# One decoder step on one core: the memory rows' squares added by VectorE in a tree, GpSimd's pooling sums behind the memory's 1/rms, seven stage slots

## What is computed

```python
h = rmsnorm(x, g_mix);  proj = h @ w_in            # columns: u (pool), q, k, v
u = proj[..., :512]
wsum[t] = sum(u[t-w+1 .. t])  for w in (2, 4, 8, 16)   # one window per 128 channels
d = wsum / count - u;  pool_out = (d @ w_pool) * s_pool
attn = softmax(q k^T) v                             # 8 heads of 64, rotary; paged cache for the 8 samples
x = x + concat(pool_out, attn) @ w_out
m = rmsnorm(memory, g_mem)                          # 256 memory rows: 1/rms = rsqrt(mean(memory^2) + eps)
mk = m @ w_ck;  mv = m @ w_cv
x = x + cross_attention(rmsnorm(x, g_cross) @ w_cq, mk, mv; cached mem_k, mem_v for the samples) @ w_co
x = x + relu(rmsnorm(x, g_mlp) @ w_up)^2 @ w_down
y = rmsnorm(x, g_final)
```

## Time and profile before

| | us |
|---|---|
| median of 3 runs | 417.19 (416.75 to 417.71) |
| the profiled execution, its own time | 417.26 |
| span of that execution in the trace | 415.2 |
| TensorE busy | 409.0 (99%) |
| VectorE busy | 253.1 (61%) |
| ScalarE busy | 226.7 (55%) |
| GpSimd busy | 31.9 (8%) |

### The profile page before, as it was taken

The page is one execution under the profiler, slowest core; times in us unless marked ns, Lnnn a source line. Parts: engine busy times, 40 slices in busy tenths (PEclk is TensorE's granted clock), DMA queues, the critical chain, the costliest instruction groups (busy, mean ns, idle before and its releaser), DMA issues.

```text
span 415.2 us, 8425 instructions
## 1 busy us (share of the span) xinstructions
PE 409.0 (99%) x3372; PEld 383.6 (92%) x3372; DVE 253.1 (61%) x400; ACT 226.7 (55%) x392; POOL 31.9 (8%) x41
## 2 busy tenths in 40 slices
PE   8999999999999999999999999999999999999995
PEld 8999979986879998957899999999999999999995
DVE  5899988576254796453259777766667534454302
ACT  5866957925364484424357666666565443453313
POOL 1004026000000120000022000000000000010010
PEclk9999999999999999999999999999999999999999
DMA  8999858974989968995537545655565555545002
GB/s 277 400 385 365 279 205 233 336 275 172 370 313 339 380 228 321 362 394 234 203 103 250 208 135 193 202 181 167 191 202 201 196 174 193 188 162 182 2 2 104
DMA packets 37257, 96.60 MB, mean 233 GB/s; under 512 B 4186, under 2 KB 13274, under 8 KB 37082
## 3 DMA queue, kind: packets, MB, share of 16 engines
q1 hardware_dynamic: 35106, 92.24, 63.5%
q10 hardware_dynamic: 2112, 3.82, 2.5%
HBM read 91.73 MB, written 4.54 MB: 232 GB/s over the span
## 4 chain that ended last, share of the span: by engine, by line
PE 85%; DVE 7%; DMA 4%; SPq 2%; issue 1%; ACT 1%; DVEq 0%
PE psum L1110 70%; PE psum L832 5%; DVE w_lo L1401 2%; PE psum L1052 2%; DMA raw<-in_w_in 2%; PE psum L960 2%; PE psum L947 2%; DMA pages<-in_page_table 1%; DMA raw<-in_w_ck 1%; SPq L778 1%; DVE mix_lo L1405 1%; PE psum L893 1%; PE psum L931 1%; ACT w_hi L1133 1%; PE psum L953 0%
## 5 line engine op out<-in xcount | busy, mean ns | idle before, releaser
L1401 DVE TENSOR_TENSOR w_lo<-raw,w_hi 128x1024 fp32r<-128x1024 f32 x67 | 82.6, 1243 | 61.0 <-ACT w_hi L1133 60.8
L1133 ACT ACTIVATE w_hi<-raw 128x1024 fp32r<-128x1024 f32 (+1 forms) x73 | 73.8, 1019 | 57.8 <-PE psum L1110 41.6
L1110 PE MATMUL psum<-mix_hi,w_hi 128*128 128x264 f32 (+1 forms) x288 | 82.4, 286 | 0.0
L1110 PE MATMUL psum<-mix_hi,w_lo 128*128 128x264 f32 (+1 forms) x288 | 81.1, 282 | 0.0
L1110 PE MATMUL psum<-mix_lo,w_hi 128*128 128x264 f32 (+1 forms) x288 | 81.1, 281 | 0.0
L1110 PE MATMUL psum<-act_hi,w_hi 128*128 128x264 f32 x232 | 66.5, 287 | 0.5 <-DVE w_lo L1401 0.5
L1110 PE MATMUL psum<-act_lo,w_hi 128*128 128x264 f32 x232 | 65.6, 283 | 0.0
L1110 PE MATMUL psum<-act_hi,w_lo 128*128 128x264 f32 x232 | 65.4, 282 | 0.0
L1110 PEld LDWEIGHTS psum<-mix_hi,w_hi 128*128 128x128 f32 x288 | 54.0, 188 | 1.0 <-issue 0.8
L1110 PEld LDWEIGHTS psum<-mix_lo,w_hi 128*128 128x128 f32 x288 | 54.0, 188 | 0.1
L1110 PEld LDWEIGHTS psum<-mix_hi,w_lo 128*128 128x128 f32 x288 | 54.0, 188 | 0.0
(11 more groups left out here) (208 smaller groups left out, 813.9 us busy)
## 6 DMA issues: line engine op xcount, KB each, us to landing
raw<-in_w_down SPq DMA_DIRECT2D x20, 512.0 KB, 3.3
raw<-in_w_up SPq DMA_DIRECT2D x18, 512.0 KB, 3.8
raw_more<-in_w_up SPq DMA_DIRECT2D x14, 512.0 KB, 3.7
stage<-in_mem_v SPq DMA_DIRECT2D x12, 512.0 KB, 6.6
raw_more<-in_w_down SPq DMA_DIRECT2D x12, 512.0 KB, 4.2
stage<-in_cache_v SPq DMA_DIRECT2D x16, 256.0 KB, 6.5
keysT<-in_cache_k SPq DMA_DIRECT2D x16, 256.0 KB, 5.4
keysT<-in_mem_k SPq DMA_DIRECT2D x8, 512.0 KB, 6.9
```

What stands on the lines that cost most here:

```text
L1110: mm = pe.matmul(out, a, b, start=first and m == 0, stop=end_ and m == 2)
L1133: return nc.scalar.activation(out, in_, ACT.Copy, scale=scale)
L1401: V.tensor_tensor(lo_of(c), raw_of(c), hi_of(c).bitcast(F32), ALU.subtract).then_inc(w_lo_ready, 1)
```

## The change

1. **Squares.** ScalarE writes the squares of the eight memory tiles into a new tile `m_squares` of eight places, with no wait for GpSimd. A new VectorE job `("sum_m",)` adds them in a tree of three instructions of 1024, 512 and 256 elements. It stands at chunk 16 behind the split. `("stat", "m")` moves from chunk 16 to chunk 17, and on ScalarE `("exp", 4)`, one head's exponentials, now comes ahead of it.
2. **GpSimd** no longer adds the memory's squares, and its four window sums wait for `rstd` of the memory (`rstd_ready` at 2) beside the take-out of the pooling columns.
3. **Seven stage slots.** All units from `V` 4 on move to another slot. The load `("mV", 1, 0, 3)` moves in SyncE's list from chunk 51 to the head of chunk 54's list, where it waits for `("xc_O", 0, 0)`, the first use of that half; `("mV", 0, 1, 3)` in the same list now waits for `("xc_O", 0, 1)`.
4. **`opart`** now lies over the constants `cos`, `sin`, `causal`, `head_q` and the pooling's counts, which have been used by then; the constants are stored in another order for this, and ScalarE's copy into it waits for the differences. With the freed slot this makes room for `m_squares`.

The core of the diff:

```diff
-STAGE = 8
+STAGE = 7
...
-    put(16, ("split",), ("stat", "m"), ("exp", 4))
-    put(17, ("m_lo", 7), ("split",))
+    put(16, ("split",), ("sum_m",), ("exp", 4))
+    put(17, ("stat", "m"), ("m_lo", 7), ("split",))
...
-    51: [("mV", 1, 0, 2), ("mV", 1, 0, 3), ("mK", 1, 2), ("mK", 1, 3)],
+    51: [("mV", 1, 0, 2), ("mK", 1, 2), ("mK", 1, 3)],
...
-    54: [("mV", 0, 1, 1), ("mV", 0, 1, 0), ("mV", 0, 1, 2), ("mV", 0, 1, 3), ("mV", 1, 1, 0), ("mV", 1, 1, 1), ("mV", 1, 1, 2), ("mV", 1, 1, 3)],
+    54: [("mV", 1, 0, 3), ("mV", 0, 1, 1), ("mV", 0, 1, 0), ("mV", 0, 1, 2), ("mV", 0, 1, 3), ("mV", 1, 1, 0), ("mV", 1, 1, 1), ("mV", 1, 1, 2), ("mV", 1, 1, 3)],
...
-        opart = sb("opart", [P, 2, CN], F32, early)
+        m_squares = sb("m_squares", [P, KT, MEM], F32, early)
+        opart = const[:, CONST_AT["cos"][0]:CONST_AT["cos"][0] + 2 * CN].rearrange("p (b n) -> p b n", b=2)
...
                     if i[0] == "x":
                         pe.wait_ge(x_summed, 1)
+                    elif i[0] == "m":
+                        pe.wait_ge(m_summed, 1)
                     else:
-                        pe.wait_ge(sq_added, (KT - 1) * m)
+                        pe.wait_ge(sq_added, (KT - 1) * (m - 1))
...
                     src = memory(k)
-                    square("m", k, src, MEM)
+                    nc.scalar.activation(m_squares[:, k, :], src, ACT.Square).then_inc(m_squared, 1)
...
+                    act.wait_ge(d_ready, len(WINDOWS))
                     copy(opart[:, OPART[job] % 2, :], B).then_inc(free, 1)
...
+                if what == "sum_m":
+                    dve.wait_ge(m_squared, KT)
+                    then(V.tensor_tensor(m_squares[:, 0:4, :], m_squares[:, 0:4, :], m_squares[:, 4:8, :], ALU.add))
+                    then(V.tensor_tensor(m_squares[:, 0:2, :], m_squares[:, 0:2, :], m_squares[:, 2:4, :], ALU.add))
+                    V.tensor_tensor(ssq[:, 1, 0:MEM], m_squares[:, 0, :], m_squares[:, 1, :], ALU.add).then_inc(m_summed, 1)
+                    return
...
-            add_squares("m")
-
             gp.wait_ge(pad_ready, 2)
             for f in range(AT):
                 wait_gemm_out(gp, group["in", 0], f)
             end_ = STATE + SEQ
+            gp.wait_ge(rstd_ready, 2)
```

More of the change, by code:

```diff
@@ L223 @@
 SCALED_BY_ACT = ()
-NO_PRODUCTS = ("m_tile", "m_lo", "differences", "square_x", "sum_x", "tables", "turn", "qblock", "k_out", "exp", "norm", "split")
+NO_PRODUCTS = ("m_tile", "m_lo", "differences", "square_x", "sum_x", "sum_m", "tables", "turn", "qblock", "k_out", "exp", "norm", "split")
 def plan_banks():
@@ L411, in host_constants @@
     parts = {
-        "cos": cos, "sin": sin, "ones": np.ones((P, P)), "eps": np.full((P, 1), EPS),
-        "causal": causal, "head_q": head_q, "head_x": head_x, "share": share,
-        "spread": spread, "inv_count": inv_count,
-        "inv_window": inv_window,
+        "ones": np.ones((P, P)), "eps": np.full((P, 1), EPS), "cos": cos, "sin": sin,
+        "causal": causal, "head_q": head_q, "inv_count": inv_count, "inv_window": inv_window,
+        "head_x": head_x, "share": share, "spread": spread,
         "ident": np.eye(P),
@@ L540, in build @@
         x_squared, x_summed = sem("x_squared"), sem("x_summed")
+        m_squared, m_summed = sem("m_squared"), sem("m_summed")
         rstd_ready, cols_ready = sem("rstd_ready"), sem("cols_ready")
@@ L1067, in sum_result @@
                 S, B = (psum[:, banks_of(len(GROUPS) - 1)[x], :] for x in (1, 2))
-                pe.wait_ge(sq_added, (KT - 1) * (m - 1) + KT - 2)
+                pe.wait_ge(sq_added, (KT - 1) * (m - 2) + KT - 2)
                 for t in range(2):
@@ L1072, in sum_result @@
                 turn_result(*Y_PARTS[0])
-                pe.wait_ge(sq_ready, KT * m)
+                pe.wait_ge(sq_ready, KT * (m - 1))
                 for t in range(2):
@@ L1147, in square @@
                 m = NORM[norm]
-                added = (KT - 1) * (m - 1) + max(k - SQ_SLOTS, 0)
+                added = (KT - 1) * (m - 2) + max(k - SQ_SLOTS, 0)
                 if added > 0:
                     act.wait_ge(sq_added, added)
-                if k == 0 and m >= 2:
+                if k == 0:
                     wait_full(act, ("stat", {2: "x", 3: "m", 4: "c"}[m]))
@@ L1690, in add_squares @@
                 m = NORM[norm]
-                n = MEM if norm == "m" else T
                 for k in range(1, KT - 1 if norm == "y" else KT):
-                    gp.wait_ge(sq_ready, KT * (m - 1) + k + 1)
+                    gp.wait_ge(sq_ready, KT * (m - 2) + k + 1)
                     if k > 1:
-                        gp.wait_ge(sq_added, (KT - 1) * (m - 1) + k - 1)
-                    nc.gpsimd.tensor_tensor(ssq[:, m % 2, 0:n], ssq[:, m % 2, 0:n], sq[:, k % SQ_SLOTS, 0:n], ALU.add).then_inc(sq_added, 1)
+                        gp.wait_ge(sq_added, (KT - 1) * (m - 2) + k - 1)
+                    nc.gpsimd.tensor_tensor(ssq[:, m % 2, :], ssq[:, m % 2, :], sq[:, k % SQ_SLOTS, :], ALU.add).then_inc(sq_added, 1)
             nc.gpsimd.memset(std[:, 0:P], 0.0).then_inc(warm_ready, 1)
```

## The result

The changed kernel takes 421.09 us, median of 4 runs (419.69, 421.04, 421.35 and 421.13 us), against 416.97 us for the kernel before in the same comparison: ratio 1.009, 95% interval 1.0073 to 1.0107. Slower, as forecast. But the median is 1.5 us above the 419.6 us predicted, and 0.1 us above the upper end of the range. (The kernel before was itself at 416.97 us here; the ratio of 1.009 on the forecast's 417.19 us would be 420.9 us.)

What follows compares the result with a forecast made beforehand. TensorE, busy for 99% of the span, was taken to bound the kernel. Terms of 0 - 0.3 + 2.1 + 0.6 = +2.4 us gave 419.6 us against the median of 417.19 us, range 418.4 to 421.0 us.

Steps and rivals of the forecast that it cites:

- What bounds the kernel: Whole kernel: TensorE, busy 99% of the span, bounds it; nothing after 57.65 us can absorb a delay of TensorE.
- GpSimd's adds go: TensorE's waits near 53 and 57.65 us: VectorE, no longer held up by GpSimd's adds, gains 0.3 us (0.2 to 0.4).
- The tree behind the split: Stat product behind chunk 17: TensorE waits for VectorE's tree behind chunk 20's split, a loss of 2.1 us (1.8 to 2.4).
- The rival without a wait: Stat product: tree done by 67.6 us, so TensorE does not wait and the kernel takes 416.9 us; chance 0.08.
- Behind the reciprocal: Chunk 20's second and third column blocks: splits alternating with window sums lose 0.15 and 0.45 us, together 0.6 (0 to 0.9).
- Seven slots and `opart`: Stage loads and ScalarE's copy into `opart`: the new waits cost 0 us, with an end at 1.0 us.
- The sum: Whole kernel: the terms add to +2.4 us, giving 419.6 us against the median of 417.19 us.
- my own sign: Behind the new wait: the forecast is wrong if TensorE's granted clock falls from 2.4 GHz; no price given.
- GpSimd first at the port: Behind the reciprocal: a window sum goes before `mix_lo` of tile 7, chunk 19 waits 1.8 us, 420.8 us; chance 0.13.
- the late load: At `xc_O(0,1)`: the moved load takes 6.0 us, not 4.7, a wait of 0.7 us, 420.3 us; chance 0.09.

Runs made afterwards that it cites:

- the first profile: Profile of the changed kernel's first of four runs against the kernel before: 419.69 us, span 417.2 us, TensorE at full clock throughout.
- the second set of runs: The changed kernel as it is, measured once more in more rounds against the kernel before: 421.75 us, ratio 1.0102.
- the long wait: The changed kernel with the memory's stat product back behind chunk 16, tree still behind the split of chunk 20: 424.43 us, ratio 1.0175.

## Why the prediction was right, and where it was not

**What bounds the kernel: right.** In the first profile TensorE's shift at 78 us is its shift at 409 us, and nothing behind absorbed or added anything. In two of the later profiles the next norm added 0.4 and 0.8 us.

**GpSimd's adds go: right, mis-sized.** 0.3 us were taken, 0.53 measured, which is also above the upper end of 0.4 us: 0.22 by the heads' transposes and the rest by O(0). That end counted the two waits that rows show. Two `w_lo` at 33 us take 2.36 us where they took 3.32, as worked out. The `uext` wait is gone, as said.

**The tree behind the split: right, and the one term that counts.** 2.1 us predicted at ends of 1.8 and 2.4, 2.05 us named by the trace, 2.30 us by the shift, so inside the ends by either. The working holds point by point: split 1.23 us, tree 2.41 us behind it, in the place that the sum gave it less the shift of 0.53 us. The rival without a wait needed the tree done by 67.6 us, 2.1 us earlier; among the kernels whose window sums still wait only those with the tree ahead of the split get there (66.15 us in the first), and that one takes 417.38 us where the rival had 416.9.

**Behind the reciprocal: right in its order, mis-sized.** `mix_lo` was first at the port, the two splits alternated with the sums. The second block lost 0.25 us (0.15 predicted). The third lost nothing (0.45 predicted). I had let the splits end at 78.75 us, less the shift 78.2, and they ended at 78.0; and I had put the third block 0.7 us behind the second, where it is 0.81 us, and TensorE came to the second 0.2 us later than in the sum. So the first `mkT` was 0.2 us early for it rather than late. Net 0.20 us in place of 0.6, inside the ends of 0 and 0.9.

**Seven slots and `opart`: right.** 0, by the run that has only these.

**The sum.** -0.53 + 2.30 + 0.20 = +1.97 us, where I had +2.4 us; with a further 0.4 us outside the span, which I had taken as unchanged, the profiled run is at 419.69 us where I had 419.7 us. Two errors of 0.4 us cancelled there.

**What the sum left out is what its last sentence names.** I named the granted clock as what would make me wrong and gave it no price, since the trace had no row at the other level. It fell in 7 of 9 runs and costs 1.5 us: by my own sign the forecast is wrong in these seven, and it is the fall that parts 419.6 us from 421.09 us (of the 2.15 us to 421.75 us it is the larger part). With a chance of its own for a fall, the range would have had to reach 422 us. As an estimate the figure could have been bounded from this case's rows: at half the clock the products of a stretch take as much again as the 0.12 us each that they took before (the profile of the second set of runs has 0.21 us), and only the length of the stretch was unknown. What I can't say even now is from the rows of before alone how likely a fall behind a wait of 2.1 us would be.

**The rivals.** GpSimd first at the port and the late load did not happen. The time that the former gave, 420.8 us, is near the measured one and for another reason.

## What to carry to other kernels

Place an addition in an in-order queue ahead of the instruction that still waits for a release: the same three instructions cost 2.3 us behind the split and nothing ahead of it. Where TensorE is the bound, price a new wait twice, for itself and for the clock behind it: here 2.05 us of wait came to some 3.5 us in most runs, a wait of 1.46 us brought the fall in 2 of 4, and 1.06 us cost only itself. A profile is one execution, so read the span and clock of every run before you take its rows for the kernel's.

## What the runs showed of the hardware that I had not expected

- TensorE's granted clock fell to its half level behind a wait of 1.46 us in 2 of 4 runs, of 2.05 us in 7 of 9, of 2.25 us in 3 of 4, of 4.88 us in 4 of 4, and behind 1.06 us or less in none of 13 (by the mean clock of each run). The fall cost 1.5 us in the three profiles that show it (4.88 and 4.89 us for 3.35, and 7.60 for 6.10); three runs behind the long wait, without a profile, took 0.8 to 1.25 us more still.
- Products of no use in the wait made the kernel faster (419.66 and 419.44 us against 421.09 and 421.75).
- A `tensor_scalar` over 8 elements per partition took 1.23 us beside a window sum and takes 0.17 us without one.
- In most runs some 0.4 us of time outside the span came with a change inside the kernel.
- At a norm that the change did not touch, TensorE waited for GpSimd's adds in two of the fourteen profiles (0.17 and 0.53 us named), and the kernel of one of them shows no such wait in its other profile.
